# Twenty-three weight chunks of a two-block transformer as three rounded products

## The chip, the cores and the metric

One Trainium2 chip, one core of it. A core has TensorE (PE, the matrix engine, with its weight loads listed apart as PEld), VectorE (DVE), ScalarE (ACT) and GpSimd (POOL), which share no program and meet only at semaphores, and a queue processor (SP) that issues most DMAs. The metric is the device time of one execution in microseconds, the median of several runs.

## The reference

Two networks run one after the other on 512 tokens of width 1024, all in float32. The first block is sparse attention, stick-breaking attention, a mixture of experts, and a last part that concerns us:

```
h3 = _rmsnorm(x, ple_norm[i])
x = x + jnp.matmul(p[i], w_ple[i]) * jax.nn.sigmoid(jnp.matmul(h3, w_ple_gate[i]))
return _rmsnorm(x, final_norm)
```

The second network puts 16 meta tokens ahead of the 512 (528 columns) and has an even and an odd layer. The even layer projects the tokens to a recurrent group (convolution, gates, a linear scan, a GELU gate) and to a latent attention of eight heads (query rank 256, key and value rank 128, a rotary part of 32). It joins both (512 + 512 features), projects them back to 1024, adds them to 4^(1/4) times the residual and takes a layer norm. An MLP with squared ReLU follows, then a retention layer and a second MLP.

## The kernel before, in words

Activations lie transposed: a tile is 128 features by 512 tokens (528 in the second network), and a matrix of 1024 rows is taken in **chunks**. A chunk is 128 x 1024 numbers (512 KB), the weights of 128 output features as eight 128 x 128 blocks, one for each k tile of the input. SP streams all chunks through a ring of eight slots (tile `weights`): the slot of chunk u is filled again once PE has begun the chunk behind its last user (semaphore `chunk_begun`), so loads are issued about six chunks ahead.

There are two ways to multiply a chunk. The **exact** way is a float32 matmul. In the profile each one shows as two rows. PE functions `linear` (L485), the gates' loop (L707) and `linear2` (L795: 528 columns as two halves of 264) do it. The other way is **three rounded products**: input x and weight w are each written as a rounded part and a remainder (`fp32r`), and PE adds wh*xh + wl*xh + wh*xl. `linear_split` (L496), `linear_parts` (L826, 512 columns) and `linear2_parts` (L809, 528 columns) do this. The parts come from the other engines:

- ACT copies a ring slot into a place for rounded weights (`high`, L1736; counts `w_hi`), and rounds the input tiles (counts `x_hi`).
- POOL subtracts the rounded weights from the ring slot in place (`low`, L2473, tile `weights_low`; counts `w_lo`).
- DVE subtracts the rounded input from the input (counts `x_lo`).
- PE takes a chunk with `take_parts`, which waits for `w_lo`.

`high` waits until the chunk that used its place before is finished, unless it is called with `slots=-1`. With two places, chunk n is rounded while PE works on chunk n-1.

The order of every engine's work is written out by hand, and each engine runs its list in that order. Around the change it is as follows. After the experts, DVE adds their output to the residual and normalizes it (`rms`, L1789); PE does eight gate chunks (L707) with the exact way; for each, ACT takes a sigmoid from PSUM (L1446), DVE multiplies and adds, ACT squares the new residual (L1449). After the final norm, PE does the entrance of the second network (L795): seven chunks, the sum of squares for the q norm (L507), two chunks, the sum for the kv norm, two chunks; then the q, k and v projections of the latents (L732), two chunks more, the gates of the recurrence, and the attention. In the attention PE alternates `scores` (L963, L966: five key tiles of a head, one head ahead) and `outputs` (L979); ACT takes five exponentials a head (L1602) and the inverse of the sums (L1610, L1611), DVE multiplies (L2313), the recurrence lies on DVE before it. The joined features are tile `Y2`: k tiles 0 to 3 from the recurrence, 4 to 7 from the heads in pairs. The output projection is eight chunks with `linear2`; in the first, k tile 4 waits for the heads. All entrances of the deep MLPs and of the first block are already three rounded products.

## Time and profile before

| what | value |
|---|---|
| median of 3 runs | 2497.31 us (2497.22 to 2499.72) |
| profiled execution, span | 2496.9 us |
| busy: PE, DVE, ACT, POOL | 95%, 33%, 29%, 27% |
| chain that ended last, by engine | PE 88%, issue 4%, DVE 3%, ACT 2%, POOL 2% |
| gates of the first layer's last part, exact | 881.6 to 938.4 us |
| entrance of the second network, exact | 945.6 to 1028.4 us, with two norm sums |
| attention of the even layer | 1069 to 1180 us |
| output projection, exact | 1179.7 to 1236.6 us |

The profiled execution's own time is its span of 2496.9 us and 0.4 us around it, if it ran like the median. A stretch of PE work that stands in the chain as one piece had no wait in it. A change of its length moves everything behind it, unless something else is late then.

### The profile page before, as it was taken

Reading aid. Unit: us, or ns where it says so; the run is one execution under the profiler, and the core shown is the slowest. Engines: PE = TensorE matmul, PEld = TensorE weight load, DVE = VectorE, ACT = ScalarE, POOL = GpSimd, SP = SyncE. Lnnn points to the kernel's source line nnn. Section 1 sums busy time; section 2 is a strip of 40 time slices with the busy share of each in tenths; the row PEclk is TensorE's granted clock in tenths of the full one; section 3 lists DMA queues with packets and bytes.
Section 4 is the critical chain, followed back from the end, with each engine's and each line's share of the span. In section 5 each row is a group of like instructions: output and inputs, shape, how many; then the busy total and the mean of one; then the engine's idle time right before and its main releaser. Section 6 shows DMA issues by size and latency. Waiting matters only on the chain.

```text
span 2496.9 us, 29386 instructions
## 1 busy us (share of the span) xinstructions
PE 2376.4 (95%) x11620; PEld 1715.4 (69%) x11620; DVE 831.4 (33%) x1298; ACT 728.9 (29%) x1089; POOL 682.1 (27%) x366
## 2 busy tenths in 40 slices
PE   7999999979999999989999999999999999999998
PEld 5585445753333347855899999979777677878875
DVE  2653412341111232350274054145000443721722
ACT  3324433321111211354142122232322334322222
POOL 3140012511111001110134444424433034544541
PEclk9699999989999999999999999999999999999999
DMA  4121111547899522200122222222222022322220
GB/s 152 60 93 59 46 37 40 229 165 273 356 358 380 237 68 72 76 18 9 59 85 85 93 86 84 93 85 94 93 85 76 18 75 69 101 85 97 97 89 38
DMA packets 68315, 275.41 MB, mean 110 GB/s; under 512 B 12488, under 2 KB 12616, under 8 KB 55920
## 3 DMA queue, kind: packets, MB, share of 16 engines
q1 hardware_dynamic: 59408, 259.61, 29.2%
q0 software_dynamic: 8512, 13.89, 1.6%
q8 instruction: 77, 1.26, 0.2%
q10 hardware_dynamic: 288, 0.40, 0.1%
q14 instruction: 30, 0.25, 0.0%
HBM read 321.02 MB, written 16.80 MB: 135 GB/s over the span
## 4 chain that ended last, share of the span: by engine, by line
PE 88%; issue 4%; DVE 3%; ACT 2%; POOL 2%; DMA 0%; DVEq 0%; POOLq 0%; SPq 0%; ACTq 0%
PE ps L826 16%; PE ps L809 15%; PE ps L1244 7%; PE ps L795 6%; PE ps L1016 4%; PE ps L1059 3%; PE ps L496 3%; PE ps L1266 3%; PE ps L1119 2%; PE ps L1205 2%; PE ps L707 2%; POOL weights_low L2473 2%; PE ps L1043 2%; PE ps L627 2%; PE ps L507 2%
## 5 line engine op out<-in xcount | busy, mean ns | idle before, releaser
L2473 POOL TENSOR_TENSOR weights_low<-weights,parts 128x1024 fp32r<-128x1024 f32 x218 | 547.3, 2513 | 988.4 <-ACT parts L1736 988.4
L826 PE MATMUL ps<-parts 128*128 128x512 f32 x1344 | 419.6, 392 | 9.2 <-DVE parts L2004 6.8
L809 PE MATMUL ps<-parts 128*128 128x264 f32 x2240 | 411.3, 285 | 8.1 <-DVE parts L2004 6.9
L1736 ACT ACTIVATE parts<-weights 128x1024 fp32r<-128x1024 f32 x218 | 229.1, 1055 | 440.4 <-PE ps L809 145.0
L809 PEld LDWEIGHTS ps<-parts 128*128 128x128 f32 x2240 | 349.6, 190 | 8.8 <-issue 8.7
L809 PE MATMUL ps<-parts,weights_low 128*128 128x264 f32 x1120 | 319.3, 285 | 0.0
L826 PEld LDWEIGHTS ps<-parts 128*128 128x128 f32 x1344 | 253.8, 189 | 66.1 <-issue 10.4
L826 PE MATMUL ps<-parts,weights_low 128*128 128x512 f32 x672 | 263.6, 392 | 0.0
L809 PEld LDWEIGHTS ps<-parts,weights_low 128*128 128x128 f32 x1120 | 213.1, 190 | 0.0
L1244 PE MATMUL ps<-area,normed 128*64 128x512 f32 x752 | 171.3, 597 | 1.6 <-DVE normed L2191 1.6
L2004 DVE TENSOR_TENSOR parts<-normed,parts 128x528 f32 (+1 forms) x64 | 152.2, 2378 | 10.1 <-DVE normed L2003 2.7
L826 PEld LDWEIGHTS ps<-parts,weights_low 128*128 128x128 f32 x672 | 127.0, 189 | 26.9
L1244 PEld LDWEIGHTS ps<-area,normed 128*64 128x64 f32 x752 | 56.0, 138 | 111.3 <-issue 109.1
L1797 DVE SCALAR_TENSOR_TENSOR residual<-residual,ps 128x528 f32<-128x528 f32 (+1 forms) x32 | 22.3, 697 | 280.9 <-PE ps L809 90.2
L1016 PE MATMUL ps<-parts 128*106 128x512 f32 (+1 forms) x320 | 100.1, 394 | 0.8 <-ACT area L1541 0.8
L795 PE MATMUL ps<-residual,weights 128*128 128x264 f32 x416 | 95.1, 391 | 2.6 <-DVE residual L1789 2.4
L795 PEld LDWEIGHTS ps<-residual,weights 128*128 128x128 f32 x416 | 80.0, 193 | 17.7 <-issue 3.8
L1316 ACT ACTIVATE area<-ps 128x512 f32<-128x512 f32 (+4 forms) x79 | 46.9, 600 | 145.6 <-PE ps L496 65.2
L1266 PE MATMUL ps<-area 128*64 128x512 f32 x376 | 87.7, 599 | 1.3 <-DVE area L2199 1.3
L1795 DVE TENSOR_TENSOR residual<-residual,ps 128x512 f32<-128x512 f32 (+1 forms) x32 | 21.5, 691 | 193.5 <-PE ps L809 86.3
L2417 POOL DMA_INDIRECT pair_rows<-normed,where x24 | 24.2, 1007 | 224.6 <-DVE normed L2205 224.6
L2002 DVE TENSOR_TENSOR parts<-normed 128x528 f32 (+1 forms) x64 | 51.4, 803 | 101.4 <-ACT normed L1751 55.6
(419 smaller groups left out, 3307.7 us busy)
## 6 DMA issues: line engine op xcount, KB each, us to landing
weights<-in_weights SPq DMA_DIRECT2D x283, 512.0 KB, 3.4
area<-in_experts SPq DMA_DIRECT2D x141, 1024.0 KB
area<-pair_rows SPq DMA_DIRECT2D x4, 1024.0 KB, 8.1
residual<-in_x SPq DMA_DIRECT2D x4, 512.0 KB, 7.2
area<-bias_scratch POOLq DMA_DIRECT2D x1, 2048.0 KB, 9.7
token_rows<-area SPq DMA_DIRECT2D x1, 2048.0 KB, 6.6
out_tiles<-residual SPq DMA_DIRECT2D x4, 512.0 KB, 2.8
area<-in_decay POOLq DMA_DIRECT2D x2, 528.0 KB, 3.7
```

The lines of the kernel that those rows point to most:

```text
L496: ins = mm(ps[:, b], wt[:, k], x[:, k], start=k == j == 0, stop=k == DT - 1 and j == 2)
L795: ins = mm(ps[:, b + h, 0:HALF], wt[:, k], rhs(m * DT + k)[:, HALF * h:HALF * h + HALF], start=m == k == 0, stop=m == len(chunks) - 1 and ...
L809: ins = mm(ps[:, b + h, 0:HALF], wt[:, k], x[:, m * DT + k, HALF * h:HALF * h + HALF], start=m == k == j == 0, stop=m == chunks - 1 and k ...
L826: ins = mm(ps[:, b], wt[:, k], x[:, m * DT + k, first:first + SEQ], start=m == k == j == 0, stop=m == chunks - 1 and k == DT - 1 and j == 2)
L1016: ins = mm(ps[0:kw, banks[j]], x[:, 2 * m + k, c:c + kw], wt[:, 512 * k:512 * k + 512], start=m == k == n == 0, stop=m == 3 and k == 1 and ...
L1059: ins = mm(ps[:, 1 + n % 6], wt[:, k], y, start=m == k == j == 0, stop=m == 1 and k == DT - 1 and j == 2)
L1244: ins = mm(ps[WIN * side:WIN * side + WIN, n % 2], XW[n % 2][:, 4 * j + k, WIN * side:WIN * side + WIN], wt, start=j == k == 0, stop=j == ...
L1266: ins = mm(ps[WIN * side:WIN * side + WIN, 4 + h], HIDT[n % 2][:, f, WIN * side:WIN * side + WIN], wt, start=f == 0, stop=f == 1)
L1736: fn(high_slot(n, place), RING[:, n % SLOTS], ACT.Copy).then_inc(S["w_hi"], 1)
L2002: v.tensor_tensor(high[:, at], f, f, ALU.mult).then_inc(S["dve_ops"], 1)
L2004: v.tensor_tensor(rest[:, at], f, high[:, at], ALU.subtract).then_inc(S["dve_evac"], 1)
L2473: g.tensor_tensor(RING_LOW[:, n % SLOTS], RING[:, n % SLOTS], high_slot(n, place), ALU.subtract).then_inc(S["w_lo"], 1)
```

## The change

Six of the eight gate chunks (2 to 7), nine of the eleven entrance chunks (2 to 10) and all eight chunks of the output projection become three rounded products. The first two gates and the first two entrance chunks stay exact. For this:

- ACT rounds the eight tiles of the input of the gates (`PH`) and of the entrance (`XHE`) and the eight of `Y2` (`YHE`), DVE subtracts (`PL`, `XLE`, `YLE`), ACT rounds 23 weight chunks, POOL subtracts 23.
- The rounded weights of gates and entrance have two places each (`IN_PLE`, `IN_EVEN`), `high` fills them as above; those of the output projection have eight (`EVOUT_AT`), so ACT can round two during the attention and six behind it.
- The output projection starts with `even_pair`: the first two chunks together, k tiles 0 to 3 of both, then 4 to 7 of both, waiting for each input tile apart.
- DVE writes the heads' meta columns after the second head, not after the last.
- On POOL a memset of one row of `KT2` moves behind the second GELU, since `XLE` lies in the same memory.

On TensorE, with the places ahead:

```diff
+        PH, PL = part(24448, DT, SEQ), part(28544, DT, SEQ)
+        IN_PLE = [[part(32640 + D * j, D) for j in range(2)], None]
+        IN_EVEN = [[part(21660 + D * j, D) for j in range(2)], None]
+        EVOUT_AT = [0, 3136] + [13212 + D * j for j in range(6)]
...
+                    if n == 2:
+                        pe.wait_ge(S["x_hi"], w.next("x_hi", DT))
+                        pe.wait_ge(S["x_lo"], w.next("x_lo", DT))
+                    if n < 2:
...
+                    else:
+                        wh, wl = take_parts(IN_PLE)
+                        for k in range(DT):
+                            for j, (wt, x) in enumerate(((wh, PH), (wl, PH), (wh, PL))):
+                                ins = mm(ps[:, b], wt[:, k], x[:, k], start=k == j == 0, stop=k == DT - 1 and j == 2)
...
-                for n in range(7):
+                for n in range(2):
                     linear2([take()], xk, DT, fresh="norm_out" if n == 0 else None)
+                pe.wait_ge(S["x_hi"], w.next("x_hi", DT))
+                pe.wait_ge(S["x_lo"], w.next("x_lo", DT))
+                for n in range(5):
+                    linear2_parts(1, tiles(XHE), tiles(XLE), IN_EVEN)
                 norm_sum(2, T2, 6, lambda t: QT2[:, t])
                 for n in range(2):
-                    linear2([take()], xk, DT)
+                    linear2_parts(1, tiles(XHE), tiles(XLE), IN_EVEN)
...
-                for n in range(8):
-                    linear2([take()], lambda k: Y2[:, k], DT, late=n == 0)
+                even_pair()
+                for n in range(6):
+                    linear2_parts(1, tiles(YHE), YLE)
...
+            def even_pair():
+                banks = [2 * bank() for _ in range(2)]
+                pair = [take_parts(IN_MLP) for _ in range(2)]
+                for side in range(2):
+                    for c in range(2):
+                        wh, wl = pair[c]
+                        for k in range(PAIRS * side, PAIRS * side + PAIRS):
+                            if c == 0:
+                                pe.wait_ge(S["x_hi"], w.next("x_hi"))
+                                pe.wait_ge(S["x_lo"], w.next("x_lo"))
+                            for h in range(2):
```

On ScalarE:

```diff
+                for t in range(DT):
+                    act.wait_ge(S["norm_out"], w.next("norm_out"))
+                    fn(PH[:, t], HA[:, t], ACT.Copy).then_inc(S["x_hi"], 1)
+                for n in range(2):
+                    high(first + n, place=IN_PLE, slots=-1)
                 for n in range(8):
                     act.wait_ge(S["tile_done"], w.next("tile_done"))
                     fn(SG2[n % 2], ps[:, 4 + n % 4], ACT.Sigmoid).then_inc(S["sg"], 1)
+                    if 2 <= n < 6:
+                        high(first + n, place=IN_PLE)
...
+                    if h == 2:
+                        for t in range(PAIRS):
+                            rounded(t, PAIRS)
+                    if h == 3:
+                        act.wait_ge(S["mla_ym"], 1)
+                        for j in range(2):
+                            high(use_of("evout") + j, slots=-1)
+                    if h in (4, 6):
+                        rounded(PAIRS + h // 2 - 2, h - 2)
...
                 inverse(HEADS - 1)
+                for j in range(2, 4):
+                    high(use_of("evout") + j, slots=-1)
+                for t in (6, 7):
+                    rounded(t, 2 * t - 6)
+                for j in range(4, 8):
+                    high(use_of("evout") + j, slots=-1)
```

On VectorE:

```diff
+                for t in range(DT):
+                    dve.wait_ge(S["x_hi"], w.next("x_hi"))
+                    v.tensor_tensor(PL[:, t], HA[:, t], PH[:, t], ALU.subtract).then_inc(S["x_lo"], 1)
...
+                    if h == 3:
+                        left(range(0, 4))
+                    if h in (4, 6):
+                        left([2 + h // 2])
+                left([6, 7])
```

On GpSimd:

```diff
+                for n in range(use_of("ple") + 4, use_of("evin")):
+                    low(n, IN_PLE)
...
+                for n in range(use_of("evin") + 2, use_of("evin") + 11):
+                    low(n, IN_EVEN)
...
+                for n in range(use_of("evout"), use_of("up0")):
+                    low(n, IN_MLP)
```

The order of the lists at two places. First ACT at the gates, before (L1312 ends the norm, L1446 is a gate's sigmoid, L1449 the square):

```order
L1312 ACTIVATE rstd<-rstd 128x512 [waits act_ops]
L1446 ACT_TABLE_LOAD
L1446 ACTIVATE area<-ps 128x512 [waits tile_done] x2
L1449 ACTIVATE area<-residual 128x512 [waits dve_evac]
L1446 ACTIVATE area<-ps 128x512 [waits tile_done]
```

and after (L1494 rounds an input tile, L1820 a weight chunk; L1499 and L1504 are the sigmoid and the square):

```order
L1358 ACTIVATE rstd<-rstd 128x512 [waits act_ops]
L1494 ACTIVATE parts<-normed 128x512 [waits norm_out] x8
L1820 ACTIVATE parts<-weights 128x1024 [waits chunk_full3]
L1820 ACTIVATE parts<-weights 128x1024 [waits chunk_full4]
L1499 ACT_TABLE_LOAD
L1499 ACTIVATE area<-ps 128x512 [waits tile_done] x2
L1504 ACTIVATE area<-residual 128x512 [waits dve_evac]
L1499 ACTIVATE area<-ps 128x512 [waits tile_done]
L1820 ACTIVATE parts<-weights 128x1024 [waits chunk_begun,chunk_full5]
L1504 ACTIVATE area<-residual 128x512 [waits dve_evac]
```

Ten roundings now stand ahead of the first sigmoid, and in gates 2 to 5 one weight rounding stands between sigmoid and square.

Second, ACT at the end of the attention, before (L1610 and L1611 are a head's inverse, L1736 rounds chunks of the MLP behind the layer norm):

```order
L1610 ACTIVATE area<-ps 64x512 [waits mla_y,mla_o]
L1611 ACTIVATE area<-area 64x512 [waits act_ops]
L1736 ACTIVATE parts<-weights 128x1024 [waits chunk_full3,lru_done]
L1736 ACTIVATE parts<-weights 128x1024 [waits chunk_full4]
L1736 ACTIVATE parts<-weights 128x1024 [waits chunk_full5]
```

and after (L1675 and L1676 are the inverse, L1820 rounds weights, L1682 tiles 6 and 7 of the joined features):

```order
L1675 ACTIVATE area<-ps 64x512 [waits mla_y,mla_o]
L1676 ACTIVATE area<-area 64x512 [waits act_ops]
L1820 ACTIVATE parts<-weights 128x1024 [waits chunk_full5]
L1820 ACTIVATE parts<-weights 128x1024 [waits chunk_full6]
L1682 ACTIVATE normed_parts<-area 128x528 [waits mla_y] x2
L1820 ACTIVATE parts<-weights 128x1024 [waits chunk_full7]
L1820 ACTIVATE parts<-weights 128x1024 [waits chunk_full0]
```

Behind the last inverse two weight chunks are rounded first, then the last two input tiles, for which DVE and then PE wait.

## Rows read from the trace of the kernel before

**Rows 1.** The page: busy time by engine, and the chain's shares.
```profile
PE 2376.4 (95%) x11620; PEld 1715.4 (69%) x11620; DVE 831.4 (33%) x1298; ACT 728.9 (29%) x1089; POOL 682.1 (27%) x366
...
PE 88%; issue 4%; DVE 3%; ACT 2%; POOL 2%; DMA 0%; DVEq 0%; POOLq 0%; SPq 0%; ACTq 0%
```

**Rows 2.** Chain in order of time: start us, length us, what.
```profile
881.62 56.76 PE ps L707 x128
...
945.63 51.77 PE ps L795 x224
...
1179.67 56.96 PE ps L795 x256
```

**Rows 3.** Stretches: length, busy PE, PEld, DVE, ACT, POOL, clock, DMA share, GB/s.
```profile
897.20:938.40 41.20, 41.16 (x96) 17.86 (x94) 11.31 (x17) 6.69 (x13) 0.00 (x0) 1.00 0.24 77
961.84:999.00 37.16, 37.16 (x168) 31.73 (x167) 0.00 (x0) 6.13 (x9) 0.00 (x0) 1.00 0.21 71
1184.00:1236.00 52.00, 52.00 (x235) 44.42 (x234) 9.99 (x13) 5.51 (x5) 9.39 (x4) 1.00 0.23 71
...
1263.78:1344.90 81.12, 81.12 (x672) 80.99 (x671) 60.22 (x45) 22.82 (x30) 40.65 (x15) 1.00 0.30 98
```

**Rows 4.** Timeline of ACT, gates and entrance: start, length, work [idle before, releaser].
```profile
897.20 0.60 ACT L1446 ACTIVATE area<-ps 128x512 f32<-128x512 f32 x1 [6.27 <-PE ps L707]
...
938.40 0.60 ACT L1446 ACTIVATE area<-ps 128x512 f32<-128x512 f32 x1 [5.75 <-PE ps L707]
...
961.84 0.61 ACT L1462 ACTIVATE area<-ps 128x528 f32<-128x528 f32 x1 [6.45 <-PE ps L795]
968.96 0.61 ACT L1462 ACTIVATE area<-ps 128x528 f32<-128x528 f32 x1 [6.51 <-PE ps L795]
```

**Rows 5.** Timeline of ACT at the kernel's own entrance.
```profile
41.20 0.60 ACT L1316 ACTIVATE area<-ps 128x512 f32<-128x512 f32 x1 [4.88 <-PE ps L496]
...
46.64 0.60 ACT L1316 ACTIVATE area<-ps 128x512 f32<-128x512 f32 x1 [3.89 <-PE ps L496]
```

**Rows 6.** The kernel's own entrance: chain, then timelines of DVE, POOL and PE.
```profile
18.85 16.84 PE ps L485 x32
...
23.26 4.89 DVE L1841 TENSOR_TENSOR parts<-normed,parts 128x512 fp32r<-128x512 f32 x8
...
25.04 7.64 POOL L2473 TENSOR_TENSOR weights_low<-weights,parts 128x1024 fp32r<-128x1024 f32 x2 [21.90 <-ACT parts L1736]
...
35.12 0.80 PE L496 MATMUL ps<-parts 128*128 128x512 f32 x1
```

**Rows 7.** Timeline of DVE ahead of the second network's entrance.
```profile
944.74 5.39 DVE L1789 SCALAR_TENSOR_TENSOR residual<-residual,vectors,rstd 128x512 f32<-128x512 f32 x8 [3.59 <-ACT rstd L1312]
```

**Rows 8.** Second layer's entrance: timelines of ACT and POOL, then PE's waits.
```profile
1695.33 0.60 ACT L1316 ACTIVATE normed<-ps 128x512 f32<-128x512 f32 x1 [4.01 <-PE ps L826]
...
1696.95 2.64 POOL L2473 TENSOR_TENSOR weights_low<-weights,parts 128x1024 fp32r<-128x1024 f32 x1 [3.16 <-ACT parts L1736]
...
PE ps L826 <- POOL weights_low L2473: 0.2, 1, 0.2
```

**Rows 9.** Attention, heads 2 to 4: timelines of PE and ACT.
```profile
1138.11 2.09 PE L963 MATMUL ps<-area 97*16 97x512 f32 x4
...
1145.72 2.09 PE L963 MATMUL ps<-area 97*16 97x512 f32 x4
...
1139.49 0.59 ACT L1602 ACTIVATE area<-ps 16x512 f32<-16x512 f32 x1
...
1145.83 0.59 ACT L1610 ACTIVATE area<-ps 64x512 f32<-64x512 f32 x1 [3.13 <-PE ps L979]
```

**Rows 10.** Attention's last inverse on ACT; in the MLP, DVE beside POOL.
```profile
1180.33 0.63 ACT L1611 ACTIVATE area<-area 64x512 f32<-64x512 f32 x1
...
1265.59 2.67 DVE L2004 TENSOR_TENSOR parts<-normed,parts 128x528 f32 x1 [0.16 <-DVE normed L2003]
...
1264.97 5.55 POOL L2473 TENSOR_TENSOR weights_low<-weights,parts 128x1024 fp32r<-128x1024 f32 x2 [47.89 <-ACT parts L1736]
```

More of the change, by code:

```diff
@@ L292, in build @@
         EARLY.update({n: IN_MERGE[0][n % 2] for n in range(use_of("wout"), use_of("wout") + 2)})
+        EARLY.update({use_of("evout") + j: part(at, D) for j, at in enumerate(EVOUT_AT)})
         XHO, XLO = part(4224, DT, N2), part(8448, DT, N2)
@@ L799, in linear2, with tiles @@
                 ins.then_inc(S["tile_done"], 1)
+            def tiles(x):
+                return [x[:, k] for k in range(x.shape[1])]
             def linear2_parts(chunks, high, low, place=IN_MLP):
@@ L1443, in body @@
                 inverse_deviation(SEQ, D, "eps1")
+                first = use_of("ple") + 4
+                w.count("norm_out", 1 + 8)
+                for t in range(DT):
[3 more added lines that the diff above has]
+                    high(first + n, place=IN_PLE, slots=-1)
                 for n in range(8):
@@ L1475, in body @@
                 squares(1, lambda t: PKV, lambda t: QT2[:, 2])
-                for j in (2, 3):
+                for n, j in enumerate((2, 3)):
                     evac2([(ALL, PREC[:, j, 3:])])
+                    high(first + 7 + n, place=IN_EVEN)
                 inverse_deviation(T2, 128, "eps2")
@@ L1614, in act_mla, with rounded @@
                 fn(WIDE_META[0:META], ps[0:META, 7, 0:P], ACT.Exp, scale=MLA_SCALE).then_inc(S["mla_p"], 1)
+                def rounded(t, done):
+                    act.wait_ge(S["lru_done" if t < PAIRS else "mla_y"], done)
+                    fn(YHE[:, t], Y2[:, t], ACT.Copy).then_inc(S["x_hi"], 1)
                 exponentials(0)
@@ L1906, in body @@
                 rms(8, SEQ, "final_norm", lambda t: XA[:, t], lambda t: XA[:, t])
+                dve.wait_ge(S["meta_in"], 16)
+                for t in range(DT):
+                    dve.wait_ge(S["x_hi"], w.next("x_hi"))
+                    v.tensor_tensor(XLE[:, t], X[:, t], XHE[:, t], ALU.subtract).then_inc(S["x_lo"], 1)
                 dve_even()
@@ L2307, in dve_even, with left @@
                         root((u - 17) // 5)
+                def left(tiles):
+                    for t in tiles:
+                        dve.wait_ge(S["x_hi"], w.next("x_hi"))
+                        v.tensor_tensor(YLE[t], Y2[:, t], YHE[:, t], ALU.subtract).then_inc(S["x_lo"], 1)
                 for j in range(4):
@@ L2448, in body @@
                 gelu(1, 1)
+                pool.wait_ge(S["mla_ones"], 1)
+                pool.wait_ge(S["gelu_in"], w.next("gelu_in", 2))
+                g.memset(KT2[96:97], 1.0).then_inc(S["mla_ones"], 1)
+                pool.wait_ge(S["mla_ones"], 2)
                 gelu(2, 13)
```

77 lines of the change are left out of this document (47 added, 30 removed).

## The prediction

> **What bounds the kernel now.** I read the busy shares first: TensorE is busy 95% of the span of 2496.9 us, the other engines about a third of it [rows 1]. A share says nothing of one stage, so next comes the chain that ended last: 88% of it is PE, and the three stretches that the change rewrites stand in it as unbroken pieces of PE work, namely the gates of the first layer's last part (56.76 us), the first seven chunks of the second block's entrance (51.77 us) and its output projection (56.96 us) [rows 2]. The table by stretches then shows PE busy for all of each stretch at a granted clock of 1.00 [rows 3]. No wait, transfer or other engine limits these stages. Shorter PE work there shortens the run one for one, as long as the work that the change gives to ScalarE (ACT), VectorE (DVE) and GpSimd (POOL) is ready in time.
>
> **The gates.** ACT evacuates a gate as soon as PE has finished it, so its rows count PE's chunks: from 897.20 to 938.40 us are six chunks, 41.20 / 6 = 6.87 us each [rows 4]. The kernel already does such a chunk as three rounded products at its entrance: evacuations at 41.20 and 46.64 us, 5.44 us [rows 5]. The tiles have the same shape (128 x 128 weights, 512 columns, eight k tiles). Gates 2 to 7 change: 6 x (6.87 - 5.44) = 8.6 us.
>
> **The entrance of the second block.** Exact chunks are 7.12 us apart (961.84 to 968.96) [rows 4]. Fourteen chunks of three products on the same 528 columns take 81.12 us in the MLP, 5.79 each; I use 5.80 [rows 3]. Nine chunks: 9 x 1.32 = 11.9 us. The two chunks behind the projections and the norm sums stay exact.
>
> **The output projection.** Eight exact chunks take 56.96 us, 7.12 each [rows 2]; with 5.80, 8 x 1.32 = 10.6 us. Together 8.6 + 11.9 + 10.6 = 31.1 us of PE work go.
>
> At 264 columns three products save less of a chunk (19%) than at 512 (21%). The MLP row shows why: weight loads (PEld) are busy 80.99 of 81.12 us there, against 31.73 of 37.16 in the exact chunks [rows 3]. So a chunk of 48 products is held by its 48 loads. The Trainium skill, "FP8 and Floating Point Precision", TensorE Precision Notes, says that true FP32 takes four passes through the array. By that rule alone three products would save a quarter, 6 x 1.72 + 17 x 1.78 = 40.6 us. The measured chunks say 31.1, and I keep those; the rule's result is a rival below.
>
> **What the products wait for at the start of a stage.** Before gate 2, ACT has to round eight tiles, DVE to subtract eight, ACT to round two weight chunks and POOL to subtract two. The kernel's own entrance is the same sequence behind the same two exact chunks. There PE started at 18.85; ACT rounded the tiles meanwhile, DVE subtracted from 23.26 to 28.15, POOL's two subtractions, which DVE's run held up, ended at 32.7 us, and the first rounded product came at 35.12, straight behind the exact ones [rows 6]. So all is ready 13.8 us after PE's start, where it is wanted after 16.3. For the gates, DVE writes the normalized tiles just ahead of PE, which starts at 881.62 as before [rows 2]: ready at 895.4 at the latest, wanted at 897.2. In fact only the DVE part (9.3 us) and the first weight chunk are wanted by then. Cost 0, and 1.7 us if POOL's second subtraction took twice as long.
>
> For the entrance, PE starts at 945.63 [rows 2]. DVE normalizes from 944.74 [rows 7], writes until 950.1, and its eight further subtractions (4.89 us for 512 columns [rows 6], so 5.0) end near 955; the first weight remainder, 2.4 to 2.8 us of POOL, follows near 958. Exact chunks 0 and 1 cover this until about 961.7. The memset of one row of KT2 on POOL is taken out of the way and runs after the second GELU; its reader, the attention, comes only after the two projections. Cost 0, bound 2 us.
>
> **What they wait for inside a stage.** With two places for rounded weights, the next chunk is prepared while the present one runs: evacuation, rounding, POOL's subtraction. The kernel does this with the same two places in the second layer: the evacuation starts at 1695.33, POOL starts at 1696.95 and ends at 1699.59, 4.26 us after the tile was done, and PE waited 0.2 us for POOL in that whole stage [rows 8]. A gate gives 5.44 us and an entrance chunk 5.80, so 1.2 and 1.5 us are left. The added rounding of a weight chunk on ACT stands ahead of the square in the gates, and one rounding ahead of the deviation of the q norm. The square is wanted only for a sum at the end of the stage, where no rounding is left (the last one is issued with gate 5), and behind the norm's sum four more chunks (23 us) follow on PE before the product that reads the q norm. Cost 0, bound 0.5 us a chunk.
>
> **The attention.** ACT gets four roundings of a tile (0.55 us each, an evacuation's time in rows 8) behind the second head's inverse, two of a weight chunk (1.05 each, what lies between evacuation and POOL there) a head later, and single ones after. In each head's period (PE's scores at 1138.11 and 1145.72, so 7.6 us) ACT waits 3.13 for the outputs [rows 9]. PE runs five score tiles ahead: the exponential of 1139.49, done at 1140.08, frees a bank that PE wants at 1145.72. 2.2 us fit in both. Cost 0; if they did not fit, 2.2 + 2.1 + 2 x 0.6 = 5.5 us.
>
> **The start of the output projection.** It is the one tight place. PE now begins with the first four k tiles of two chunks, 48 products = 5.8 us, and then wants tiles 4 to 7, one each 0.73 us. It starts near 1179.6 as before [rows 2] and wants tile 7 at 1187.6. ACT finishes the last inverse at 1180.96 [rows 10], then rounds two weight chunks (2.1) and tiles 6 and 7, until 1184.2. DVE can subtract tile 7 at once if it is free of POOL, so from 1184.8 (no stall). But POOL gets two weight subtractions at 1182.1. The MLP's rows show how such a pair meets DVE: POOL 5.55 us for two, and the DVE operation beside it 2.67 instead of 0.7, as each waits for the other's end [rows 10]. So tile 6 comes at 1185.2 and tile 7 at 1188.2: a stall of 0.6 us. Ends: 0 (POOL held instead, as at the entrance [rows 6]) and 3.4 (one more subtraction of 2.7 ahead). I take 0.6, the alternation of the MLP's rows. The Trainium skill, "GPSIMD Engine Reference", Specifications, states that GpSimd shares its SBUF interfaces with VectorE and that operations with two SBUF inputs contend; the rows agree.
>
> **Loads.** A ring chunk is loaded six chunks ahead, and stretches of 5.8 us a chunk run in the MLP at a DMA share of 0.30 with no wait [rows 3]. Cost 0.
>
> **Sum.** 31.1 - 0.6 = 30.5 us less than the span: 2466.4. The median of the runs shown, 2497.31, is 0.4 above it, so 2466.8 us.
>
> **Rivals.**
> 1. The forecast, 2465.5 to 2468.5. Chance 0.75.
> 2. The covers fail in places: the pair at the projection (3.4), the attention (5.5), a start (1.7 or 2), and some handoffs. Two or three together cost 3 to 8 us: 2470 to 2475. For it speak the port shared by DVE and POOL and ACT's new load; against it the entrance and the second layer, which carry the same patterns with no wait. Chance 0.16.
> 3. Slower. If the chunk's handoff (ACT, then POOL) is not beside the present chunk but behind it, each of the 23 chunks waits 4.26 us [rows 8]: 98 - 31 = 67 us slower, 2564. It decides once the chain is longer than a chunk by 1.35 us (31.1 / 23), so above 6.8 us in the gates and 7.1 in the others. POOL held up by DVE as at the entrance (3.8 us each [rows 6]) makes it 5.7, which costs little. Chance 0.02.
> 4. No change: if the freed PE time came back as waits for the ring or at the stages' ends. The unchanged stages are tied to PE's end alone, and the 30% of DMA speaks against. 2495 to 2499, chance 0.03.
> 5. A quarter of each chunk goes, 40.6 us: 2456.7. It would need faster products than any in this trace. This is the four-pass rule of the Trainium skill's page on floating point. Chance 0.04.
>
> The range of 80% is 2464 to 2472: the forecast with its unknowns, and the lower half of rival 2. About 0.2% (5 us) is what a measurement of this kernel can tell from no change. Faster by more: 1, 2 and 5, 0.95; within: 0.03; slower: 0.02.
>
> **What would show it.** In the profile after, the gates' evacuations 5.44 us apart from the third to the eighth, the entrance's 5.80 apart (the norm sums between), the projection about 47 us long; products of the gates directly behind the exact ones; PE waiting for DVE's last remainder by under 1 us at the projection's eighth tile; the attention's period still 7.6 us. Wrong it would be if PE waited for POOL's weight remainders in every chunk, if the period of the attention grew, or if a granted clock below 1.00 stood in a rewritten stretch behind its first chunk.

## The result and the profile after

| | before | after |
|---|---|---|
| time, median | 2498.51 us (4 runs, 2497.22 to 2499.81) | 2471.86 us (4 runs, 2469.68 to 2476.98) |
| ratio after / before | | 0.9895, 95% interval 0.9882 to 0.9908 |
| profiled execution, span | 2496.9 us | 2469.3 us (its time 2471.07 us) |

The change made the kernel 26.7 us faster. The forecast had 30.5 us and a time of 2466.8; its range ended at 2472. The span became 27.6 us shorter, 2.9 us less than forecast, and the forecast had put only 0.4 us around the span of before, where the profiled execution after has 1.8 us.

The busy shares of the page and the chain's shares answer [rows 1]. PE's share stays at 95%: the run is still PE's.

```profile
PE 2348.8 (95%) x11940; PEld 1722.2 (70%) x11940; DVE 873.0 (35%) x1322; ACT 763.5 (31%) x1136; POOL 745.6 (30%) x389
...
PE 88%; issue 4%; DVE 3%; ACT 2%; POOL 2%; DMA 0%; DVEq 0%; POOLq 0%; SPq 0%; ACTq 0%
```

The chain of after, in order of time, answers [rows 2]. L727, L854 and L820 are the rounded products, L720 and L837 the exact chunks that stayed.

```profile
881.55 15.62 PE ps L720 x32
897.17 32.70 PE ps L727 x144
938.76 16.17 PE ps L837 x64
954.93 29.21 PE ps L854 x240
985.92 11.67 PE ps L854 x96
998.48 11.68 PE ps L854 x96
...
1163.92 4.39 DVE branch_parts L2402 x2
1168.44 3.90 PE ps L820 x30
1172.34 35.03 PE ps L854 x288
...
1234.78 81.22 PE ps L854 x672
```

Six gates take 32.70 us, 5.45 each. Five entrance chunks take 29.21 us, 5.84 each. The products stand directly behind the exact chunks (897.17, 954.93), so the covers at both starts hold. In the output projection one piece of DVE work has come into the chain.

The stretches answer [rows 3], with the same columns. All four run at a granted clock of 1.00 with PE busy throughout. In the three on 528 columns PEld is as busy as PE (81.0 of 81.2 us or closer), as the forecast read from the MLP.

```profile
902.70:929.90 27.20, 27.16 (x120) 22.16 (x118) 18.72 (x15) 9.37 (x15) 11.06 (x4) 1.00 0.32 97
960.82:984.18 23.36, 23.36 (x193) 23.35 (x192) 0.00 (x0) 8.71 (x12) 9.58 (x4) 1.00 0.28 92
1172.34:1207.37 35.03, 35.03 (x289) 35.03 (x289) 13.32 (x12) 5.53 (x5) 15.69 (x7) 1.00 0.29 93
1234.78:1316.00 81.22, 81.20 (x673) 80.99 (x671) 60.22 (x45) 22.80 (x30) 40.64 (x15) 1.00 0.32 98
```

The timelines of ACT and, in the second fence, of POOL inside the two stages answer [rows 4] and [rows 8]. An evacuation comes every 5.44 us in the gates and every 5.84 us in the entrance, and POOL is done at 970.69, 4.03 us after the evacuation of 966.66 began.

```profile
902.70 0.60 ACT L1499 ACTIVATE area<-ps 128x512 f32<-128x512 f32 x1 [4.37 <-PE ps L727]
...
929.90 0.60 ACT L1499 ACTIVATE area<-ps 128x512 f32<-128x512 f32 x1 [4.32 <-PE ps L727]
...
966.66 0.61 ACT L1517 ACTIVATE area<-ps 128x528 f32<-128x528 f32 x1 [1.79 <-PE ps L854]
```

```profile
968.30 2.39 POOL L2582 TENSOR_TENSOR weights_low<-weights,parts 128x1024 fp32r<-128x1024 f32 x1 [3.43 <-ACT parts L1820]
```

So the three edited stages give nearly what was forecast. The rest went between them. The first fence is PE's timeline of before, from the sum of squares behind the gates to the entrance; the second is the same place after.

```profile
941.29 1.10 PE L876 MATMUL ps<-rstd,matrices 128*128 128x512 f32 x2 [2.93 <-DVE rstd L1804]
942.23 1.02 PE L878 MATMUL ps<-area,matrices 128*128 128x512 f32 x2
945.63 2.85 PE L795 MATMUL ps<-residual,weights 128*128 128x264 f32 x7 [2.39 <-DVE residual L1789]
```

```profile
932.79 2.04 PE L921 MATMUL ps<-rstd,matrices 128*128 128x512 f32 x2 [2.93 <-DVE rstd L1888]
934.63 1.75 PE L923 MATMUL ps<-area,matrices 128*128 128x512 f32 x2
938.76 2.71 PE L837 MATMUL ps<-residual,weights 128*128 128x264 f32 x7 [2.39 <-DVE residual L1873]
```

The two waits for DVE are equal (2.93 and 2.39 us), but the sum's two matmuls take 2.04 and 1.75 us in place of 1.10 and 1.02. The windows show why. The granted clock is given there as a share of full speed. Columns: stretch, its length, PE's busy time, granted clock, DMA share, GB/s. The first is before, the second after.

```profile
938.00:948.00 10.00, 4.68 (x12) 0.91 0.05 5
948.00:958.00 10.00, 10.00 (x43) 0.92 0.48 172
...
1648.00:1658.00 10.00, 7.39 (x32) 1.00 0.17 54
```

```profile
930.00:940.00 10.00, 4.82 (x9) 0.80 0.00 0
940.00:950.00 10.00, 10.00 (x40) 0.85 0.44 142
...
1315.00:1325.00 10.00, 6.55 (x34) 0.67 0.19 54
...
1618.00:1628.00 10.00, 6.87 (x24) 0.83 0.15 52
```

The clock record of each trace holds only two levels, 1.2 and 2.4 GHz. Before, one stretch at 1.2 GHz fell on this place; after, two did. At the second layer's norm (1648 before, 1618 after) the trace of before has none, the one of after has one.

For all kernels I split the span at the first matmul of the same stages. These are differences of start times in PE's timelines, in us; only the column "scores" ends where the last matmul of its stage starts. "Sum" is the sum of squares, "narrow" all from the projections of the latents to the first score. "Head" is all before the gates, which no edit of the parts touches (the kernels with names in e, w and s add a few matmuls there); "behind scores" is the rest of the attention and the output projection.

| kernel | head | gates | sum | entrance | narrow | scores | behind scores | layer norm, MLP 0 | layer 1 to MLP 1 | MLP 1 | end |
|---|---|---|---|---|---|---|---|---|---|---|---|
| before | 881.6 | 59.67 | 4.34 | 82.75 | 41.07 | 30.72 | 136.29 | 400.0 | 463.8 | 375.2 | 21.5 |
| after | 881.6 | 51.24 | 5.97 | 71.23 | 41.06 | 30.75 | 125.41 | 400.1 | 465.0 | 375.6 | 21.5 |
| b_gates | 882.3 | 51.11 | 5.90 | 82.75 | 41.07 | 31.08 | 136.18 | 401.2 | 465.0 | 375.7 | 21.5 |
| c_entrance | 880.7 | 59.66 | 4.34 | 71.25 | 41.07 | 30.72 | 134.67 | 401.0 | 465.0 | 375.6 | 21.5 |
| d_outproj | 881.8 | 59.74 | 4.34 | 82.75 | 41.07 | 30.73 | 126.69 | 397.4 | 464.9 | 375.6 | 21.5 |
| e_three | 881.9 | 49.57 | 4.34 | 69.52 | 41.07 | 45.66 | 128.56 | 397.4 | 464.9 | 375.5 | 21.5 |
| w_before | 883.1 | 58.10 | 4.34 | 81.06 | 41.06 | 30.75 | 136.30 | 394.4 | 463.7 | 370.9 | 21.5 |
| w_after | 884.1 | 49.60 | 4.34 | 69.54 | 41.06 | 30.74 | 130.24 | 394.4 | 463.4 | 370.8 | 21.5 |
| w_gates | 883.0 | 49.57 | 4.34 | 81.06 | 41.06 | 46.43 | 140.69 | 394.3 | 463.4 | 370.8 | 21.5 |
| s_before | 882.2 | 58.10 | 4.34 | 81.07 | 41.07 | 30.73 | 134.66 | 394.3 | 463.8 | 370.8 | 21.5 |
| s_after | 884.3 | 49.57 | 4.34 | 69.51 | 41.06 | 30.74 | 126.78 | 394.3 | 463.4 | 370.8 | 21.5 |
| s_gates | 883.1 | 49.57 | 4.34 | 81.06 | 41.07 | 31.08 | 132.99 | 394.3 | 463.4 | 370.8 | 21.5 |
| s_order | 879.4 | 49.59 | 4.34 | 69.52 | 41.06 | 30.74 | 126.10 | 394.4 | 463.4 | 370.8 | 21.5 |

Read across the two first rows: gates -8.43, sum +1.63, entrance -11.52, behind scores -10.88, layer 1 +1.23, MLP 1 +0.42, together -27.6.

### The profile page after: what moved, and what is told of

Same layout as the page of the kernel before. It is cut to its first block, busy times and chain, and to the rows that moved or that the text cites. A ratio compares the mean times of both kernels' runs of the same rounds, so it can differ in the third digit from the quotient of the medians.

```text
span 2469.3 us, 30143 instructions
## 1 busy us (share of the span) xinstructions
PE 2348.8 (95%) x11940; PEld 1722.2 (70%) x11940; DVE 873.0 (35%) x1322; ACT 763.5 (31%) x1136; POOL 745.6 (30%) x389
## 4 chain that ended last, share of the span: by engine, by line
PE 88%; issue 4%; DVE 3%; ACT 2%; POOL 2%; DMA 0%; DVEq 0%; POOLq 0%; SPq 0%; ACTq 0%
PE ps L854 18%; PE ps L871 16%; PE ps L1290 7%; PE ps L1062 5%; PE ps L505 4%; PE ps L1105 4%; PE ps L1312 3%; PE ps L1165 2%; PE ps L1251 2%; POOL weights_low L2582 2%; PE ps L1089 2%; PE ps L636 2%; PE ps L516 2%; PE ps L727 1%; PE ps L1229 1%
## 5 line engine op out<-in xcount | busy, mean ns | idle before, releaser
L2582 POOL TENSOR_TENSOR weights_low<-weights,parts 128x1024 fp32r<-128x1024 f32 x241 | 610.3, 2536 | 1044.8 <-ACT parts L1820 1044.7
L854 PE MATMUL ps<-parts 128*128 128x264 f32 x2384 | 452.0, 286 | 8.1 <-DVE parts L2095 6.9
L871 PE MATMUL ps<-parts 128*128 128x512 f32 x1344 | 419.7, 393 | 9.0 <-DVE parts L2095 6.8
L1820 ACT ACTIVATE parts<-weights 128x1024 fp32r<-128x1024 f32 x241 | 252.6, 1055 | 429.5 <-PE ps L854 146.6
L854 PEld LDWEIGHTS ps<-parts 128*128 128x128 f32 x2384 | 376.7, 190 | 8.7 <-issue 8.7
L854 PE MATMUL ps<-parts,weights_low 128*128 128x264 f32 x1120 | 319.5, 285 | 0.0
L871 PEld LDWEIGHTS ps<-parts 128*128 128x128 f32 x1344 | 254.1, 189 | 65.7 <-issue 10.3
L854 PEld LDWEIGHTS ps<-parts,weights_low 128*128 128x128 f32 x1120 | 213.3, 190 | 0.0
L1879 DVE TENSOR_TENSOR residual<-residual,ps 128x512 f32<-128x512 f32 (+1 forms) x32 | 21.5, 690 | 192.3 <-PE ps L854 85.1
L1312 PE MATMUL ps<-area 128*64 128x512 f32 x376 | 87.7, 599 | 1.3 <-DVE area L2290 1.3
L2030 DVE TENSOR_TENSOR area<-ps,area 106x512 f32<-106x512 f32 (+4 forms) x20 | 9.3, 479 | 201.3 <-PE ps L1078 201.3
L505 PE MATMUL ps<-parts 128*128 128x512 f32 x256 | 79.8, 392 | 0.7 <-ACT area L1405 0.7
```

What stands on the lines that cost most here:

```text
L505: ins = mm(ps[:, b], wt[:, k], x[:, k], start=k == j == 0, stop=k == DT - 1 and j == 2)
L854: ins = mm(ps[:, b + h, 0:HALF], wt[:, k], x[m * DT + k][:, HALF * h:HALF * h + HALF], start=m == k == j == 0, stop=m == chunks - 1 and k ...
L871: ins = mm(ps[:, b], wt[:, k], x[:, m * DT + k, first:first + SEQ], start=m == k == j == 0, stop=m == chunks - 1 and k == DT - 1 and j == 2)
L1312: ins = mm(ps[WIN * side:WIN * side + WIN, 4 + h], HIDT[n % 2][:, f, WIN * side:WIN * side + WIN], wt, start=f == 0, stop=f == 1)
L1820: fn(high_slot(n, place), RING[:, n % SLOTS], ACT.Copy).then_inc(S["w_hi"], 1)
L2582: g.tensor_tensor(RING_LOW[:, n % SLOTS], RING[:, n % SLOTS], high_slot(n, place), ALU.subtract).then_inc(S["w_lo"], 1)
```

## The experiments

### The parts alone

First the changed kernel again (no edit), then each of its three parts with the other two undone on every engine. On PE the gates are undone so (left out in b_gates):

```diff
-                    if n == 2:
-                        pe.wait_ge(S["x_hi"], w.next("x_hi", DT))
-                        pe.wait_ge(S["x_lo"], w.next("x_lo", DT))
-                    if n < 2:
+                    if n < 8:
                         wt = take()
```

The entrance (left out in c_entrance) and the output projection (left out in d_outproj):

```diff
-                for n in range(5):
-                    linear2_parts(1, tiles(XHE), tiles(XLE), IN_EVEN)
+                for n in range(7):
+                    linear2([take()], xk, DT, fresh="norm_out" if n == 0 else None)
...
-                even_pair()
-                for n in range(6):
-                    linear2_parts(1, tiles(YHE), YLE)
+                for n in range(8):
+                    linear2([take()], lambda k: Y2[:, k], DT, late=n == 0)
```

**a_again.** 

> The changed kernel once more, unaltered, beside the kernel before. Its first runs gave a time 26.7 us below before, where the forecast had 30.5; in the profile the three rewritten parts gave 8.4, 11.5 and 9.7 us (29.6 together), and 2.0 us went where nothing was edited. Theory 1 (clock): the 2.0 us are stretches at a stage's start in which the granted clock is low, and they come in most runs at the places where they came first (the sums of squares behind the gates, the first exact entrance chunk): time 25.5 to 28 us below before, span ends 27 to 28 us earlier, last gate sigmoid to first entrance matmul 8.9 us against 7.2 in before. Theory 2 (noise of one run): the time comes out at 29 to 31 us below before, and 7.2 us from the last sigmoid to the entrance. Theory 3 (a later stage is slowed for good by the edits): stages behind the output projection stand longer than in before in this run too, by the same 1 to 2 us at the same places.

2471.95 us (2469.51 to 2473.90, 4 runs), before 2498.86: ratio 0.9892, 0.9877 to 0.9907. That is 26.9 us, the first result again. Theory 2 falls: it is not the noise of one run. The low clock stood at the same places as in the first profile. Theory 3 is taken up below.

**b_gates.** 

> Only the six gate chunks as three products; entrance and output projection exact as in before (the one moved memset of the keys' row stays moved). The part by itself: six pitches of 5.44 us for 6.87, so the last gate sigmoid 8.4 us earlier. Theory 1 (the low clock behind the gates comes from how the gate stage ends): 1.6 us are given back between the last sigmoid and the entrance's start, time 6 to 7.5 us below before. Theory 2 (noise): 8.4 to 8.8 us below. Theory 3 (loss in later stages made by the other parts): 8.4 to 8.8 below, and the loss is seen in the runs of the other parts.

Median 2494.90 us, 4.0 below before. The ratio, which takes all eleven runs together, is 0.9999 (0.9981 to 1.0017), so this part alone is not shown to be a gain. Nine of its eleven runs lie between 2493.39 and 2497.21, two at 2512.8 and 2512.9, with a granted clock of 0.962 over the span. The gates' stage is 8.56 us shorter, as expected, and in the profiled run 5.4 us went elsewhere: 0.7 in the head, 1.6 in the sum, 0.4 in the scores, 1.2 in the first MLP, 1.2 in the second layer and 0.5 in the second MLP (less 0.1 gained behind the scores), all stages without an edit. Every theory had expected a larger gain, and theory 1 had looked for the loss in the sum alone. It is spread wider.

**c_entrance.** 

> Only the nine entrance chunks as three products; gates and output projection exact. The part by itself: nine pitches of 5.84 us for 7.12, so first entrance matmul to first latent projection 11.5 us shorter. Theory 1: the start of the entrance is as in before, since the gates are, so the whole 11.5 us arrives: time 10.5 to 12.5 us below before. Theory 2: 11.5 to 12. Theory 3: below 10.5, because the stages from the scans to the attention stand longer.

2488.65 us, 10.2 below before (ratio 0.9961, 0.9947 to 0.9974). The entrance is 11.50 us shorter, the sum is unchanged at 4.34. The gain lies 0.3 us short of theory 1's range and 1.3 short of theory 2's, where theory 3 had put it. But the stages that theory 3 named, from the scans to the attention, are not longer (narrow 41.07, scores 30.72, both as in before). Gained were 1.0 in the head and 1.6 behind the scores, lost 1.0 in the first MLP, 1.2 in the second layer and 0.4 in the second MLP.

**d_outproj.** 

> Only the output projection as three products (with the rounding of the attention's outputs on ScalarE and the subtractions on VectorE beside the attention); gates and entrance exact. The part by itself: eight pitches of 5.84 us for 7.12 less a stall of 0.4 us, 9.7 us. Theories 1 and 2: the attention's period stays 7.62 us and the time is 9.2 to 10.2 us below before. Theory 3 (the added work in the attention, or the nine weight subtractions on GpSimd beside VectorE's, holds up a later stage): 7 to 8.5 us below, with a longer attention or a later start of the layer norm.

2488.21 us, 10.65 below (0.9956, 0.9943 to 0.9970), more than its stage's 9.60 and above the expected 9.2 to 10.2. The profiled run got 2.6 us in MLP 0, where its trace has less of the low clock than that of before, and lost 1.2 in the second layer. So the clock gives as well as takes. The three parts' medians add up to 24.8 us, their stages to 29.7. For theory 3, that an edit slows later work for good, nothing speaks: the stages that it would act on (narrow, scores) are equal to 0.4 us, and in the others the change has both signs. The kernels with filled gaps below say it more strongly: in them these other stages have the same length with the edits and without.

### Filling TensorE's idle gaps

What decides where the clock falls? In the trace of after, each low stretch from 860 us to the last layer norm stands at or just behind an idle gap of PE of 2.4 to 3.5 us, except one in the attention. The Trainium skill, "TensorE: Matmul & The Clock Gate", Part 1, says that the array's clock is halved by a monitor of its recent activity, and the places of these stretches agree with that. So these kernels give PE work on constants in the gaps, whose result nobody reads:

```diff
+            def warm(full, half=0, b=0):
+
+                for n in range(full + half):
+                    width = 512 if n < full else 256
+                    mm(ps[:, b, 0:width], ONES, CM[:, 0:4].rearrange("p a b -> p (a b)")[:, 0:width], start=True, stop=True)
...
                 begin_stage("dve_evac", 4)
+                warm(2)
                 for n in range(8):
...
                 w.count("dve_evac", 8)
+                warm(2, 1)
                 begin_stage("dve_evac")
                 rms_sum(MERGED[:, DT - 1])
+                warm(2)
```

**e_three.** 

> The changed kernel with 6.5 extra matmuls on constants (512 columns, exact fp32, bank 0, result never read) in the three idle gaps of TensorE around the gates: two before the first gate, two and a half before the sum of squares behind the gates, two before the entrance. The gaps measured 2.4, 2.9 and 2.4 us and one such matmul takes 1.02 us at full clock, so they should fit. Theory 1 (an idle gap of TensorE draws a low stretch on what stands behind it): granted clock 1.00 at 882 to 888, 933 to 939 and 939 to 945 us, the sum of squares back from 2.04 and 1.75 us to 1.0 and 1.0, the two exact entrance chunks back from 16.2 to 14.3 us; time 3.5 to 5 us below the changed kernel's 2472, near 2467.5. Theory 2 (the low stretches fall at random or with the start of a stage, whatever TensorE did before): clocks as before, time 2472 plus up to 0.5 for the extra work.

PE's timeline at the same place (L925 is the added work):

```profile
928.39 2.31 PE L925 MATMUL ps<-matrices 128*128 128x512 f32 x6
931.48 1.10 PE L930 MATMUL ps<-rstd,matrices 128*128 128x512 f32 x2 [0.79 <-DVE rstd L1897]
932.41 1.02 PE L932 MATMUL ps<-area,matrices 128*128 128x512 f32 x2
933.27 1.88 PE L925 MATMUL ps<-matrices 128*128 128x512 f32 x4
935.82 6.47 PE L840 MATMUL ps<-residual,weights 128*128 128x264 f32 x28 [0.67 <-DVE residual L1882]
```

The local part of theory 1 holds: the sum's matmuls are back at 1.10 and 1.02 us, the gates' stage went from 51.24 to 49.57, the sum from 5.97 to 4.34, the entrance from 71.23 to 69.52, 5.0 us together. The total does not: 2481.42 us in the median, ratio 0.9921 (0.9898 to 0.9945). One of six runs had 2463.74, the others 2480.55 to 2486.02. In the profiled one the score stage took 45.66 us in place of 30.75. The forecast of that time, 2467.5, was wrong: I had not seen this second behaviour coming. I call runs with it "of the second kind". Only the profiled run shows the stage itself; the other four of the five are put there by their times and by the clock of 0.965 to 0.966 over their spans, where the run of 2463.74 has 0.975.

**w_after.** 

> The changed kernel with such matmuls in every idle gap of TensorE over 2.4 us from 421 us on that has a free bank: before the merge, around the gates as in the run beside it, behind three layer norms, and in the four places of the feed-forward blocks where the second product waits 3.4 us for VectorE. Theory 1: of the low stretches behind 421 us about twelve go, each worth 0.9 to 1.7 us by what the rows at either clock differ: time 2452 to 2460, granted clock of the span 0.98 or more. Theory 2: 2472 to 2474.

The further places: before the merge, behind the layer norms (`warm(2, 1, 5)`), and in both MLPs before the second product:

```diff
+                    pe.wait_ge(S["act_evac"], w.value("act_evac", 3))
+                    warm(3)
                     begin_stage("dve_evac")
                     with pe_loop(2, 8, dve_evac=4, w_lo=8):
```

2459.96 us (2458.35 to 2470.22, 4 runs), ratio 0.9856 (0.9838 to 0.9874), at the upper end of the expected 2452 to 2460. The highest of the four, 2470.22, has a span clock of 0.970 where the others have 0.979; it has no profile, but looks like one of the second kind. Its windows, with the columns as above, at five of the filled places:

```profile
931.00:941.00 10.00, 8.54 (x28) 1.00 0.11 25
941.00:951.00 10.00, 10.00 (x47) 1.00 0.50 163
...
1315.00:1325.00 10.00, 9.10 (x60) 1.00 0.18 54
...
1614.00:1624.00 10.00, 9.02 (x37) 1.00 0.15 52
...
2346.00:2356.00 10.00, 9.21 (x35) 1.00 0.18 55
```

All ten windows at gaps read 1.00; in after they read 0.67 to 0.85. MLP 0's stretch is 5.7 us shorter, MLP 1's 4.8.

**w_before.** 

> The kernel before with the same extra matmuls in the same gaps. Theory 1: 11 to 18 us below the kernel before, and the difference between this run and the changed kernel with the same matmuls is what the edits themselves are worth, 29 to 30.5 us, not 26.7. Theory 2: no gain, difference 26 to 28 us. Theory 3 (a part of the change slows a later stage): difference 26 to 28 us although both show the high clock.

2485.81 us (2482.98 to 2487.85), 12.5 below before (0.9949, 0.9936 to 0.9962). Its filled stages come to the lengths that they have in w_after (MLP 0 394.4 and 394.4, layer 1 463.7 and 463.4, MLP 1 370.9 and 370.8), whatever they were before the filling. At this equal clock the gates are 8.50 us apart (58.10 and 49.60) and the entrance 11.52 (81.06 and 69.54). The medians differ by 25.9 us, though, less than the expected 29 to 30.5 and just under the 26 to 28 of theories 2 and 3. What speaks against both is the stages: the profiled w_after spends more time at the low clock behind the scores (130.24 us for the stage, 126.78 in s_after) and has a head 0.9 us longer, 4.4 us together.

**w_gates.** 

> Only the gate chunks as three products, with the same extra matmuls in the same gaps. Without them this part by itself was 4.0 us below the kernel before in the median, although its stage is 8.4 us shorter. Theory 1 (the 4.4 us were lost to low clock in stages behind it): 8 to 9 us below the kernel before with the same matmuls, and no runs that are 18 us longer. Theory 3 (the gates' edit makes later work slower in another way): 4 to 5 us below it.

Median 2495.12 us, ratio 0.9952 (0.9926 to 0.9977), 12 runs of two kinds: four at 2472.7 to 2473.0, one at 2481.4, seven at 2494.2 to 2498.4 (span clock 0.969 to 0.971). The first kind is 13 us below w_before, 4.5 more than its stage gives; the profiled run is of the second kind, so where these 4.5 came from is not shown. In s_gates below, of the first kind, no low stretch stands behind the scores and that part is 3.3 us shorter than in w_before, which would be most of it. The second kind is 8 to 13 us above w_before. The expectation that no such runs would come was wrong.

### The score stage

In the runs of the second kind the score stage of the second block's attention runs at the low clock from its third microsecond to its end and some 5 to 11 us beyond. It is made of short matmuls that wait for DVE's maximum two tiles back. These kernels add half a matmul ahead of the first score and behind the last score of each head:

```diff
+                warm(0, 1, 6)
...
                     ins.then_inc(S["logits"], 1)
+                    if t == 4:
+                        warm(0, 1, 6)
```

**s_after.** 

> The changed kernel with the extra matmuls of w_after and, in the score stage of the second block's attention, half a matmul (256 columns, 0.5 us) ahead of the first score and one behind the last score of each head, where TensorE waits 0.8 us. In the runs so far that stage took either 30.7 us at full clock or 45.7 to 46.4 us at a granted clock of 0.50 from its second or third microsecond on, and runs of the second kind were 15 to 20 us longer. Theory 1 (idle time at the stage's start draws the low clock, which then stays): no run of the second kind, score stage 30.7 to 31.5 us, all runs 2457 to 2463. Rival (the stage's low clock has nothing to do with idle time, or the extra work itself brings it): runs of both kinds as in w_after, or the stage is longer by up to 8 times 0.3 us.

**s_before.** 

> The kernel before with the same extra matmuls, those in the score stage too. Theory 1: 2483 to 2488, no run of the second kind, and s_after is 26 to 30 us below it: 29.6 by the stages, less 3.5 where the attention behind the scores draws one low stretch more in one of them. Rival: the edits are worth under 26 us at equal clock.

**s_gates.** 

> Gate chunks alone as three products, with the same extra matmuls. Seven of the twelve runs of w_gates were of the second kind (2494 to 2498), four were at 2472.7. Theory 1: no run of the second kind, 8 to 13 us below s_before. Rival: still half of the runs near 2496.

s_after: 2456.65 us (2450.48 to 2458.32, 5 runs), ratio 0.9824 (0.9812 to 0.9837), no run of the second kind; three of its runs are below the expected 2457 to 2463. s_before: 2484.28 (2483.96 to 2486.44), 0.9945 (0.9932 to 0.9958). s_gates: median 2475.39, ratio 0.9930 (0.9908 to 0.9953), eight of eleven runs at 2472.8 to 2477.0, three at 2493.5 to 2496.6; its median is 8.9 us below s_before, what the gates' stage gives (8.53). s_after is 27.6 us below s_before, inside the expected 26 to 30; its profiled run has a head longer by 2.2 us and one low stretch more behind the scores. So the added work did not remove the second kind; it came in three of eleven runs where it had come in seven of twelve, too few to call the difference shown. Theory 1, that idle time at the stage's start draws the low clock, had expected none and is not borne out. The stage itself, from its windows in w_gates (second kind) and in s_gates (first):

```profile
1059.00:1105.42 46.42, 40.43 (x96) 22.30 (x96) 20.91 (x87) 18.96 (x28) 7.63 (x8) 0.53 0.00 0
```

```profile
1059.15:1090.23 31.08, 28.02 (x109) 15.10 (x110) 21.11 (x87) 18.97 (x28) 7.67 (x8) 1.00 0.00 0
```

DVE and ACT do the same work in both (21 and 19 us); PE's takes 40 us in place of 28, and the stage is 15.3 us longer. The added halves cost nothing: the stage took 30.74 us in s_after and in w_after.

**s_order.** 

> As s_after, and behind the last head's inverse ScalarE rounds the attention tile 6, a weight chunk, tile 7, a weight chunk, where it did two weight chunks and then both tiles. The output projection's TensorE wait for the subtraction of tile 6 was 0.42 us. If that wait hangs on ScalarE's order it goes: 0.3 to 0.5 us less between the first matmul of the output projection and its last. If it hangs on the last head's output it stays. The total can't tell 0.4 us; the profile does.

```diff
-                for j in range(2, 4):
-                    high(use_of("evout") + j, slots=-1)
-                for t in (6, 7):
-                    rounded(t, 2 * t - 6)
+                for t, j in ((6, 2), (7, 3)):
+                    rounded(t, 2 * t - 6)
+                    high(use_of("evout") + j, slots=-1)
```

The wait in the projection is in PE's timeline of s_after, and s_order has no wait of PE in that stretch. It is the wait for k tile 7, not 6: 66 products stand ahead of it, 48 for tiles 0 to 3 of two chunks and 18 for tiles 4, 5 and 6.

```profile
1167.56 0.36 PE L827 MATMUL ps<-normed_parts,parts 128*128 128x264 f32 x1 [0.43 <-DVE branch_parts L2420]
```

From its first matmul to its last the projection takes 46.66 us against 47.33, and the whole stage 126.10 against 126.78, both with the same low stretches behind the scores. So the wait hung on ACT's order. It was worth 0.67 us, more than the expected 0.3 to 0.5, which counted the idle time alone (see the stall below). The time, 2457.63 (2452.53 to 2464.00), can't tell it from s_after, as expected.

## Why the prediction was right or wrong

**What bounds it.** Right. PE stood alone in the three stretches, and each became shorter by what its chunks did.

**The gates, 8.6.** 8.43 in the first profile, 8.53 at an equal clock (58.10 less 49.57). The pitch of 5.44 us was exact.

**The entrance, 11.9.** 11.52. **The output projection, 10.6 less a stall of 0.6.** 9.60 with both at two low stretches (136.29 less 126.69). The pitch was mis-sized: 5.84 us where I had rounded the MLP's 5.79 up to 5.80; over seventeen chunks that is 0.7 us. The stall was there, at the tile named and from the cause named. PE was idle 0.42 us, but the first product behind the wait starts 0.71 us after the one ahead of it, where products here start 0.12 apart, so the stall cost 0.59, the forecast's 0.6. s_order gives 0.67 for it (PE's timeline, then DVE's):

```profile
1167.73 0.28 PE L820 MATMUL ps<-branch_parts,parts 128*128 128x264 f32 x1
1168.44 0.36 PE L820 MATMUL ps<-normed_parts,parts 128*128 128x264 f32 x1 [0.42 <-DVE branch_parts L2402]
```

```profile
1163.92 4.38 DVE L2402 TENSOR_TENSOR branch_parts<-area,normed_parts 128x528 fp32r<-128x528 f32 x2 [1.87 <-ACT normed_parts L1682]
```

DVE's two subtractions took 4.38 us beside POOL; the one for tile 5, without it, took 0.69. Together the stages give 29.6 of 30.5.

**The covers at the starts, cost 0.** Right. The preparation of the gates ran like the kernel's own entrance [rows 6], with POOL held up by DVE in the same way: 8.08 us for two (7.64 there), done at 895.8, which is 0.4 us behind the latest time that the forecast gave, and wanted at 897.2 and later.

```profile
885.97 4.90 DVE L1985 TENSOR_TENSOR parts<-normed,parts 128x512 fp32r<-128x512 f32 x8
```

```profile
887.74 8.08 POOL L2582 TENSOR_TENSOR weights_low<-weights,parts 128x1024 fp32r<-128x1024 f32 x2 [36.93 <-ACT parts L1820]
```

**The handoff inside a stage, the attention, the loads, cost 0.** Right. The handoff took 4.03 us of 5.84, the attention's period is 7.62 us as before, the scores take 30.75 us for 30.72. The rounding of a tile took 0.64 us, not 0.55: the rows that the prediction names for it show 0.60. It changed nothing.

**The sum.** This is the step that failed. It read "30.5 us less than the span", with all that was not edited kept as it was. The unedited stages do keep their work and their waits, but not their granted clock: low stretches at the idle gaps cost 1.6 us more in the sum, 1.2 in the second layer and 0.4 in MLP 1, and 1.3 us less in the attention, 2.0 us net. The prediction had put this term at nothing without a reason. The filled gaps show the cause for the gap places: the same stages came back to the same length in every kernel with them. That the clock falls at a given gap in one kernel and not in another with the same gap was seen (layer 1: 463.8 in before, 465.0 in after), and what picks it was not tested. The attention's part has no experiment made for it, but the runs sort by it: with the exact projection, the part behind the scores takes 132.99 us with no low stretch (s_gates), 134.66 and 134.67 with one (s_before, c_entrance), 136.29 with two (before); with the rounded one 125.41 with one (after) and 126.69 with two (d_outproj).

**0.4 us around the span.** Mis-sized. I took the median of the runs shown for the time of the profiled execution. Later runs of before have 2498.82 us with a span of 2497.1, so 1.7 us lie around it, and 1.3 of the miss is this. With it the same sum gives 2468.1. The median's miss of 5.0 us is then 0.9 in the edited stages, 2.0 at the clock, 1.3 around the span, and 0.8 by which the profiled run lies below the median of after. That the time still fell inside the range to 2472, by 0.1 us, is owed to the width that failed covers had given it, not to a cause that it named.

**The rivals.** 3, 4 and 5 did not come. Rival 5 wanted a quarter of each chunk gone; 21% (6.87 to 5.44) and 18% (7.12 to 5.84) went. Rival 2 named a cost of the right size, but by failed covers; no cover failed. None of the rivals held the clock, though the prediction named a clock below 1.00 as something that would prove it wrong in the edited stretches. I looked for it there only.

## What to carry to other kernels

When a forecast subtracts a stage's gain from the span, list the idle gaps of TensorE in the stages behind it, and read the granted clock there: gaps of 2.4 to 3.5 us here made the work behind them some 1.6 us longer or not, and a change of start times rearranged which did. Filling such gaps with matmuls on constants into a free bank removed it, and was worth half as much as the change itself, but runs in which the score stage stayed at the low clock came with it (five of six of e_three, seven of twelve of w_gates). With that stage filled too they were none of five in s_after and still three of eleven in s_gates. s_after stands at 2456.65 us, 15 us below the changed kernel and 42 below the kernel before. Take the time around the span from an execution whose span and time are both known.

## What the runs showed of the hardware

- A granted clock that falls in a stage of short, dependent matmuls can stay low to the stage's end: scores 46.4 us in place of 31.1 (w_gates and s_gates, profiled runs), and runs of one kernel over 21 us apart (2472.7 and 2494 to 2498 for w_gates). How often it came, judged by time and span clock where there is no profile: in none of five runs each of c_entrance, d_outproj, w_before, s_before, s_after and s_order, in one of four of w_after, two of eleven of b_gates, three of eleven of s_gates, seven of twelve of w_gates, five of six of e_three. What decides it stays open: on PE the score stage of w_gates is that of w_before to the instruction.
- The head of the kernel, the same instructions in s_after and s_order, took 884.3 and 879.4 us in two executions. Both traces record 85.3 us at the low clock there. Set side by side matmul by matmul, s_after falls behind in steps: 1.2 us at 19 to 23 us, 2.1 at 538 to 541, 0.9 at 559 to 566 and 0.6 at 865. At the second of them the clock fell at 539.6 us in s_after and at 541.4 in s_order, which was 1.3 us further on in the same work. So at this step, at least, what differs is which work of PE the low clock falls on. A difference of 5 us between two single profiles is no evidence of an edit.
- A rounded weight subtraction costs POOL 2.39 us alone and 4.04 beside DVE's run of eight.
